# Split projections chunk by chunk, with retention between the attention projections, in a hybrid attention and mixture-of-experts block

## What is computed

```
mod = c @ w_ada + b_ada                 -> sh1, sc1, gt1, sh2, sc2, gt2
h   = rmsnorm(x) * (1 + sc1) + sh1
proj = h @ w_in                         # 1024 x 4688, columns:
   qa ka va (512 each), qi (1024), ki (64), wi (16), qb kb vb gb (512 each)
y_a: attention, 8 heads of 64; an indexer (16 heads: relu(qi.ki) weighted by wi) scores all keys,
     each query keeps its 256 best keys and takes a softmax over them
y_b: retention, 8 heads of 64: rotary q and k, decayed causal scores inside a tile, a state carried
     from tile to tile, group norm per head, times silu(gb)
x   = x + gt1 * (concat(y_a, y_b) @ w_o)
h   = rmsnorm(x) * (1 + sc2) + sh2
x   = x + gt2 * moe(h)                  # 32 experts in 4 groups, top 2; silu(h Wg) * (h Wu) @ Wd
out = rmsnorm(x)
```

## Time and profile before

| | |
|---|---|
| median of three runs | 1815.68 us |
| the profiled execution | 1816.96 us, its span 1815.1 us |
| busy: PE, DVE, ACT, POOL | 1577.2, 1083.7, 870.3, 273.1 us |
| mean granted TensorE clock | 0.932 of full speed |
| first float32 projection starts | 49.95 us |
| scoring starts | 186.7 us |
| second projections start | 290.1 us |
| last projection ends | 742.7 us |
| experts | from about 1090 us |

### The profile page before, as it was taken

The page is one execution under the profiler, slowest core; times in us unless marked ns, Lnnn a source line. Parts: engine busy times, 40 slices in busy tenths (PEclk is TensorE's granted clock), DMA queues, the critical chain, the costliest instruction groups (busy, mean ns, idle before and its releaser), DMA issues.

```text
span 1815.1 us, 20481 instructions
## 1 busy us (share of the span) xinstructions
PE 1577.2 (87%) x6918; PEld 1053.4 (58%) x6918; DVE 1083.7 (60%) x1498; ACT 870.3 (48%) x1181; POOL 273.1 (15%) x212
## 2 busy tenths in 40 slices
PE   2999899999999999867888984399999999999950
PEld 2446454444445555525666654378888888888840
DVE  6323796331233467353344424599999999999946
ACT  4000577778523300132344430177777777777722
POOL 0000010100021112100000000123232232323115
PEclk8899999999999999858999986599999999999985
DMA  9059743201100000321112110599999999999937
GB/s 375 16 189 376 269 154 136 81 4 44 47 6 7 6 7 12 110 85 47 59 61 69 42 47 23 196 390 397 405 401 400 399 398 397 398 395 399 385 142 275
DMA packets 85378, 346.97 MB, mean 191 GB/s; under 512 B 10048, under 2 KB 14272, under 8 KB 60736
## 3 DMA queue, kind: packets, MB, share of 16 engines
q1 hardware_dynamic: 56384, 268.51, 38.2%
q10 hardware_dynamic: 17024, 41.95, 6.0%
q0 software_dynamic: 11904, 35.66, 5.5%
HBM read 295.75 MB, written 58.72 MB: 195 GB/s over the span
## 4 chain that ended last, share of the span: by engine, by line
PE 79%; DVE 8%; ACT 3%; DMA 3%; issue 3%; POOL 2%; SPq 0%; DVEq 0%; POOLq 0%; ACTq 0%
PE PS L1522 16%; PE PS L1631 12%; PE PS L1470 11%; PE PS L1472 11%; PE PS L1471 11%; PE PS L1557 4%; PE PS L1760 2%; PE PS L1580 1%; PE PS L1656 1%; PE PS L1669 1%; DVE wlo L1393 1%; DVE WK L931 1%; PE PS L1735 1%; DMA WK<-in_w_ada 1%; PE PS L1542 1%
## 5 line engine op out<-in xcount | busy, mean ns | idle before, releaser
L1393 DVE TENSOR_TENSOR wlo<-raw,whi 128x2048 fp32r<-128x2048 f32 x192 | 435.7, 2284 | 34.0 <-ACT whi L844 33.6
L844 ACT ACTIVATE whi<-raw 128x2048 fp32r<-128x2048 f32 x192 | 363.8, 1913 | 116.6 <-DVE WK L1412 81.1
L1522 PE MATMUL PS<-BIG 128*128 128x512 f32 (+1 forms) x640 | 238.9, 528 | 1.1 <-ACT WK L726 1.1
L1631 PE MATMUL PS<-BIG 128*128 128x512 f32 x512 | 224.1, 599 | 0.7 <-ACT KV L713 0.7
L1470 PE MATMUL PS<-whi,xhi 128*128 128x512 f32 x512 | 203.9, 398 | 7.3 <-DVE wlo L1393 6.5
L1472 PE MATMUL PS<-whi,xlo 128*128 128x512 f32 x512 | 201.1, 393 | 0.0
L1471 PE MATMUL PS<-wlo,xhi 128*128 128x512 f32 x512 | 200.1, 391 | 0.0
L1522 PEld LDWEIGHTS PS<-BIG 128*128 128x128 f32 x640 | 110.2, 190 | 112.4 <-issue 110.5
L1631 PEld LDWEIGHTS PS<-BIG 128*128 128x128 f32 x512 | 97.6, 192 | 122.5 <-issue 120.3
L739 ACT ACTIVATE KV<-ACC,WK 128x1024 int8<-128x1024 f32 (+4 forms) x160 | 147.1, 923 | 31.3 <-DVE WK L1036 31.3
L617 POOL COPY wcol<-tw 128x1 f32 (+1 forms) x32 | 63.0, 1969 | 376.8 <-DVE WK L1430 376.8
(11 more groups left out here) (289 smaller groups left out, 2326.6 us busy)
## 6 DMA issues: line engine op xcount, KB each, us to landing
raw<-in_w_gate SPq DMA_DIRECT2D x64, 1024.0 KB, 7.1
raw<-in_w_up SPq DMA_DIRECT2D x64, 1024.0 KB, 7.8
raw<-in_w_down SPq DMA_DIRECT2D x64, 1024.0 KB, 7.4
y_dram<-zero ACTq DMA_DIRECT2D x8, 3072.0 KB, 13.9
BIG<-in_w_in SPq DMA_DIRECT2D x8, 2048.0 KB, 10.8
WK<-in_w_ada POOLq DMA_DIRECT2D x16, 1024.0 KB, 7.4
y_dram<-WK ACTq DMA_DIRECT2D x32, 512.0 KB, 6.7
BIG<-in_w_ada SPq DMA_DIRECT2D x3, 2048.0 KB, 18.5
```

The costliest lines, as they stand in the source:

```text
L844: nc.scalar.activation(whi[:, slot], raw[:, q], ACT.Copy).then_inc(G("m_hi"), 1)
L1393: V.tensor_tensor(wlo[:, slot], raw[:, q], whi[:, slot].bitcast(F32), ALU.subtract)\
L1522: last = mm(PS[:, u % 4, 0:w], hT[:, k, tile(t)], weights[:, k, 0:w], start=(k == 0), stop=(k == KD - 1))
L1631: last = mm(PS[:, k, :], hT[:, d, tile(t)], wb[k][:, d, :], start=(d == 0), stop=(d == KD - 1))
```

## The change

The input projections now all read split parts, except kiwi. hT is split once, in place (`hT_lo` over hT, `hT_hi` beside it). The chunks come in the order kiwi, qi0, qi1, then after scoring qb, kb, vb, gb, then qa, va, ka. Each chunk's 2 MB of weights are loaded, split by ACT (`split_high`) and DVE (`split_low`) in four pieces each at a fixed unit of the chunk before, and used by all 8 tiles. The retention inputs are finished per unit (rotated, or copied, or silu) into four buffers `EV` and stored to `b_dram`. Retention itself runs tile by tile in the 24 steps of qa, va and ka: three parts per tile (turn and evacuate; scores, kv and mask; values and finish), with its rows read back from `b_dram`. The counting steps of the key search spread over both stages, and its pieces are spent in the last 16 steps. Stores of qa rows move from POOL's queue to SP's. The late w_ada loads start after unit 16 rather than 8.

```diff
-CHUNKS_A = (("qi0", ...), ("qi1", ...), ("kiwi", 2560, 80), ("qa", ...), ("ka", ...), ("va", ...))
-CHUNKS_B = (("qb", 2640), ("kb", 3152), ("vb", 3664), ("gb", 4176))
+CHUNKS = (("kiwi", 2560, 80), ("qi0", 1536, 512), ("qi1", 2048, 512), ("qb", 2640, 512), ("kb", 3152, 512),
+          ("vb", 3664, 512), ("gb", 4176, 512), ("qa", 0, 512), ("va", 1024, 512), ("ka", 512, 512))
+INDEX, RETAIN, ATTEND = 0, 3, 7
+STEP_SPEND = 4.0
+        slots = [(WK[:, 5904:10000], WKR[:, 5904:10000], ACCR[:, 0:4096]), y_slot, y_slot, x_slot, y_slot, x_slot, y_slot,
+                 x_slot, (KV[:, 0:4096],) + x_slot[1:]]
+        def bank_of(u):
+            return u % 2 if u >= FIRST[ATTEND] else u % 4
 # SP
+            load_weights(0)
             ... w_ada loads ...
+            load_weights(1)
+            sp.wait_ge(G("xt_ready"), T)
+            load_weights(2)
+            sp.wait_ge(G("a_proj"), FIRST[RETAIN])
+            load_weights(3)
+            sp.wait_ge(G("sc_ready"), NU)
+            load_weights(4)
+            for n in range(RETAIN, ATTEND):
+                if n > RETAIN:
+                    sp.wait_ge(G("a_proj"), T * n)
+                    load_weights(n + 1)
+                for t in range(T):
...
+                    sp.dma_start(b_dram[n - RETAIN, tile(t), :], EV[m % 4]).then_inc(G(f"st_ev{m % 4}"), 16)
+            for step in range(3 * T):
+                t, part = divmod(step, 3)
+                if part == 2 and t < T - 1:
+                    sp.wait_ge(G("b_kv"), t + 1)
+                    load_rows("q", 0, t + 1)
+                    load_rows("k", 1, t + 1)
+                if part == 0 and t > 0:
+                    sp.wait_ge(G("b_y"), t)
+                    load_rows("v", 2, t)
+                    store_retained(t - 1)
+                    load_rows("g", 3, t)
+                if 1 <= step <= T:
+                    sp.wait_ge(G("a_evac"), TURN1 + step)
...                                                   # q_dram store
+                if step == T:
+                    sp.wait_ge(G("a_proj"), T * (ATTEND + 1))
+                    load_weights(ATTEND + 2)
 # ACT
+            def split_high(n):
+                act.wait_ge(G(f"ld_w{n % 3}"), 16 * (n // 3 + 1))
+                if n == ATTEND + 2:
+                    act.wait_ge(G("a_proj"), T * n)
+                raw_, _, hi = W[n]
+                for k in range(0, KD, 2):
+                    own.go(A(hi[:, k:k + 2], raw_[:, k:k + 2], ACT.Copy), G("w_hi"))
+            hidden_high(0)
+            for u in range(TURN1):
                 a_copy(u)
+                if u == 1:
+                    split_high(1)
+                if u == 3:
+                    hidden_high(1)
+                if u == T + 4:
+                    split_high(2)
...
+                if u == NU // 2:                      # inside scoring
+                    split_high(RETAIN)
...
+            for step in range(3 * T):
+                t, part = divmod(step, 3)
+                a_copy(FIRST[ATTEND] + step)
+                if part == 0:
+                    b_evacuate(t)
+                if step == 3:
+                    split_high(ATTEND + 1)
+                if step == 2 * T - 1:
+                    split_high(ATTEND + 2)
+                count_some(2)
 # DVE
             for m in range(TURN1):
                 a_rotate(m)
                 if m >= 1:
                     a_evacuate(m - 1)
+                if m == 2:
+                    split_low(1)
+                if m == 4:
+                    hidden_low(0)
+                if m == T + 1:
+                    hidden_low(1)
+                if m == T + 6:
+                    split_low(2)
...                                                   # scoring, then
+            split_low(RETAIN)
+            for u in range(FIRST[RETAIN], FIRST[ATTEND]):
+                n, t = divmod(u, T)
+                if n < RETAIN + 2:
+                    b_rotate(u)
+                if t == 4:
+                    split_low(n + 1)
+                narrow_some(1 + u % 2)
+            pieces = select()
+            for step in range(3 * T):
+                t, part = divmod(step, 3)
...
+                if name != "va":
+                    a_rotate(m)
+                narrow_some(2)
+                if step == 5:
+                    split_low(ATTEND + 1)
+                if step == 2 * T - 1:
+                    split_low(ATTEND + 2)
+                if (1 <= step <= T) or step > 2 * T:
+                    a_evacuate(m - 1)
+                if part == 1:
+                    b_mask(t)
...
+                if part == 2:
+                    b_finish(t)
+                if step >= T:
+                    spend(STEP_SPEND, pieces)
 # PE
+            def project(u):
...
+                    if t == 0 and k % 2 == 0:
+                        pe.wait_ge(G("w_lo"), 4 * (n - 1) + k // 2 + 1)
+                    _, w_lo, w_hi = W[n]
+                    last = split_product(out_, hT_hi[:, k, tile(t)], hT_lo[:, k, tile(t)], w_hi[:, k], w_lo[:, k],
+                                         first, final)
+            for step in range(3 * T):
+                t, part = divmod(step, 3)
+                m = TURN1 + (step if step <= T else step - T)
+                project(FIRST[ATTEND] + step)
+                if (1 <= step <= T) or step > 2 * T:
+                    a_turn(m - 1)
+                if step == 3 * T - 1:
+                    a_turn(m)
...
+                    query_keys(0, 0)
+                (retain_turn, retain_scores, retain_values)[part](t)
```

More of the change, by code:

```diff
@@ new lines, in _, with store_retained @@
+            sp.wait_ge(G("a_proj"), T * ATTEND)
+            load_weights(ATTEND + 1)
+            for j in range(4):
+                sp.wait_ge(G(f"st_ev{j}"), 16 * 8)
+            load_rows("g", 3, 0)
+            def load_queries(n):
+                sp.dma_start(queries(n), q_dram[:, :, tile(n)]).then_inc(G(f"ld_q{n % 2}"), 16)
+            def store_retained(t):
+                sp.wait_ge(G("b_out"), t + 1)
+                sp.dma_start(yb_dram[tile(t), :], WB["y"]).then_inc(G("st_yb"), 16)
@@ L697, in zero_rows, with hidden_high @@
                     .then_inc(G(f"st_y{h}"), 16)
+            def split_high(n):
[5 more added lines that the diff above has]
+                    own.go(A(hi[:, k:k + 2], raw_[:, k:k + 2], ACT.Copy), G("w_hi"))
+            def hidden_high(half):
+                part = slice(512 * half, 512 * half + 512)
+                for k in range(KD):
+                    act.wait_ge(G("hT_ready"), KD * half + k + 1)
+                    own.go(A(hT_hi[:, k, part], hT[:, k, part], ACT.Copy), G("hT_hi"))
             def a_copy(u):
-                name, _, w = CHUNKS_A[u // T]
+                name, _, w = CHUNKS[u // T]
                 t = u % T
@@ L994, in a_rotate, with split_low, hidden_low @@
                     own(rotate_part(v, t, 8), G("a_rot"))
+            def split_low(n):
+                raw_, lo, hi = W[n]
+                for k in range(0, KD, 2):
+                    dve.wait_ge(G("w_hi"), 4 * (n - 1) + k // 2 + 1)
+                    own.go(V.tensor_tensor(lo[:, k:k + 2], raw_[:, k:k + 2], hi[:, k:k + 2].bitcast(F32), ALU.subtract),
+                           G("w_lo"))
+            def hidden_low(half):
+                part = slice(512 * half, 512 * half + 512)
+                dve.wait_ge(G("a_proj"), 4 * half + 4)
+                for k in range(KD):
+                    dve.wait_ge(G("hT_hi"), KD * half + k + 1)
+                    own.go(V.tensor_tensor(hT_lo[:, k, part], hT[:, k, part], hT_hi[:, k, part].bitcast(F32),
+                                           ALU.subtract), G("hT_lo"))
             for m in range(TURN1):
@@ L1153, in b_retain, with b_mask @@
+            def b_mask(t):
                 dve.wait_ge(G("b_s"), t + 1)
@@ L1213, in _ @@
+            for _ in pieces:
+                pass
             for kind, i in order:
@@ L1534, in _ @@
-            a_project(range(NA1))
+            def project(u):
+                n, t = divmod(u, T)
+                w = CHUNKS[n][2]
+                out_ = PS[:, bank_of(u), 0:w]
+                if bank_before(u) is not None:
+                    pe.wait_ge(*evacuated(bank_before(u)))
+                if u == 0:
+                    pe.wait_ge(G("ld_w0"), 16)
+                for k in range(KD):
+                    first, final = k == 0, k == KD - 1
+                    if n == 0:
+                        if t % 4 == 0:
+                            pe.wait_ge(G("hT_ready"), KD * (t // 4) + k + 1)
+                        last = mm(out_, hT[:, k, tile(t)], W[0][:, k, :], start=first, stop=final)
+                        continue
+                    if n == 1 and t % 4 == 0:
+                        pe.wait_ge(G("hT_lo"), KD * (t // 4) + k + 1)
+                    if t == 0 and k % 2 == 0:
[3 more added lines that the diff above has]
+                                         first, final)
```

(6 more changed lines are left out.)

372 lines of the change are left out of this document (157 added, 215 removed).

## The result

The changed kernel takes **1749.28 us** (median of four executions, 1747.59 to 1750.48) where the kernel before took 1814.45 beside it: ratio 0.9642, 95% interval [0.9625, 0.9659]. The forecast was 1739, with four fifths of the chance between 1705 and 1773. The profiled execution took 1747.59 us, its span 1745.8.

What follows compares the result with a forecast made beforehand. TensorE's work was taken as the bound up to about 743 us. The last projection ending 56.6 us earlier and a tail 20.2 shorter gave -76.8; 1816.96 less 76.8 and 1.3 made 1739, with 1705 to 1773 leaving out a fifth.

Steps and rivals of the forecast that it cites:

- Rival 5: Wide projection units: three passes bring no gain at 0.286 us a pass, giving 1841 us; chance 0.01.
- rival 4: Attention part: short waits hold TensorE's clock down over its 24 units, costing 131 us, giving 1870; chance 0.04.
- the third case: Attention part: DVE and ACT coupled tighter, POOL lock added, about five tiles slip 5 us each: 1764; chance 0.19.
- Landmark 1: Start of scoring: first wide unit at 79.3, scoring from 176.6 us instead of 186.7, which is -10.1.
- the term of 2.8: Inside scoring: the new split_high stops ACT for 4.2 us, buffered rows cover 1.4, so +2.8 us (0 to 4.2).
- The 2.7 put on a cold restart: First b units after scoring: the idle stretch cools TensorE's clock, +2.7 us (0 to 2.7).
- Landmark 3: End of the last projection, after b chunks and attention part: 686.1 us instead of 742.7, with 26.6 of stalls.
- mask(4): Attention part: DVE's mask for retention tile 4 comes 5.3 us late for TensorE.
- Landmark 4: From last projection to first late row: 23 us (20 to 30) instead of 43.2, -20.2; after it 0.
- the first case: The forecast itself, stalls as worked: 1739 us, own range 1722 to 1752; chance 0.57.
- Rivals 2 and 3: Stalls around TensorE: mostly covered, 1710 us (chance 0.19), or DVE and ACT coupled tighter, 1764 us (chance 0.19).
- Rival 2: Scoring and attention part: stalls mostly covered, 3.5 us for 19.6 and several others nothing: 1710; chance 0.19.

Runs made afterwards that it cites:

- E4: Changed kernel with a fourth pass (low part of rows by low part of weights) in each wide unit: 1852.4 us, 1.0219 of the kernel before.
- E11: Changed kernel with one float32 product of the high parts in place of three passes, splits kept: 1821.09 us, 1.0046 of the kernel before.
- E1: Changed kernel with the eight zero stores moved into the b chunks, every third unit: 1740.69 us, 0.9578 of the kernel before.
- E7: Changed kernel with unused 128x512 float32 products ahead of and among the kiwi units: 1746.63 us, 0.9629 of the kernel before.
- E0: The changed kernel run again, unedited, as common ground for the experiments: 1748.41 us, 0.9639 of the kernel before.
- E2: Changed kernel with 2.5 instead of 4.0 nominal units of selection pieces per attention-projection step: 1730.17 us, 0.9538 of the kernel before.
- E3: Changed kernel with ACT's split of the first b weights behind scoring instead of in its middle: 1742.78 us, 0.9608 of the kernel before.
- E6: Changed kernel with the edits of E1, E2, E3 and no selection pieces ahead of chunk ka's split: 1722.53 us, 0.9490 of the kernel before.
- E9: E6 with the tile's mask ahead of DVE's two narrowing steps in the qa part: 1717.86 us, 0.9455 of the kernel before.
- E5: Changed kernel with all eight retention tiles in a stage of their own behind ka: 1788.16 us, 0.9840 of the kernel before.

## Why the prediction was right, and where it was not

**The unit.** 5.46 us from 24 passes of 0.227; measured 5.44. E4 and E11 price the term from both sides: 1.81 more a unit for the fourth pass, 73 us for all 72 units back to float32. Rival 5 is out, and so is rival 4: the clock was 0.99 in the b chunks and 0.93 in the attention part. A kb unit, beside which the third case had put the waits of DVE and POOL for each other, takes 5.44 as well. By the Trainium skill (TensorE: Matmul & The Clock Gate, "The HAM clock gate") activity releases the throttle; at 5.44 us a unit the trace agrees.

**Landmark 1 is the step that failed:** "176.6, which is -10.1" was 0.0. I counted for each new or moved instruction what it waits for, but took the unchanged ones as unchanged. The eight zero stores are not in the diff's arithmetic at all, yet they are tied to units that became 1.4 us shorter. E1 shows it by taking them away (6.2 us), E4 and E11 by lengthening the unit (their issues are short again). E1 leaves 3.9 of the 10.1: 1.3 at the first wide unit (80.6 there for 79.3) and 2.6 behind it, about 2 of them the cold start told below. The Trainium skill (DMA: Bandwidth & Descriptors, "Issuing engines are not separate DMA queues") calls the time an issue takes on its engine "usually small relative to the DMA itself". That holds for the kernel before (0.38 of a median 13.9 us from issue to landing); at 13.44 against 22.6 it doesn't, and the measurement decides.

The start within landmark 1 came out near, but for one reason more than I gave. I had kiwi done near 68, which needs the upper clock from about its third unit on, with DVE's chain setting 79.3. In fact kiwi ran at 0.50 throughout and TensorE itself was busy until 80.2. DVE's chain came out as worked (half of hT's low part 70.82 to 75.71, the rotation behind it done at 76.5), so the two nearly tied (TensorE waited for DVE for only 0.74 us, at 76.5), and with the clock up E7 shows DVE's alone at 77.7. The cold start of the first wide unit, about 2 us (clock 0.50 until 84.2), was missing. On the sentence about activity and the throttle this chunk is the exception: 28.71 us busy of 30 left the clock at 0.50.

**Scoring.** 110.8 from its start to the first qb unit, measured 111.0. That close a hit is luck: with the same code up to there E0 took 109.4 and E2 113.9. E3 confirms the term of 2.8 inside it. The 2.7 put on a cold restart there is not separated from it by any run.

**Landmark 3.** From the first qb unit to the last projection I had 398.7 us, 367.4 of work and 31.3 of stalls and clock. Measured 395.8: idle times sum to 18.1 (the three shown of that stretch and four under 0.8), and the other 10.3 are work at the lower clock (377.7 busy for 367.4). The parts were partly off. The gap at ka was 7.5 and not 12.4, as DVE's lag was smaller; mask(4) was 5.2 late for 5.3; the counts cost 3.7 for 3. E2 removes the one at mask(4), E6 halves the one at ka, and E9 moves the one from the counts. For the clock behind long gaps I had put 3; over this stretch E2 gave back 5.6 beside 5.4 of gaps.

**Landmark 4.** 19.1 us for 23, inside its range: values, finish and late rows overlap more than in my list. Behind it I had put 0, bound 3. The changed kernel's profiled execution takes 1033.2 us there for the 1029.2 of the kernel before, but E0, the same kernel, takes 1028.9. So the 0 stands within what moves between executions; why this stretch moves stays open. The clock was 0.50 from 710 to 750, and in the kernel before from 769 to 819.

**The sum.** 1749.28 is 10.3 over the forecast, about the 10.1 of landmark 1. It lies in the first case's own range of 1722 to 1752, near its end, and that is in part luck: the stores were no term of any case, and the range was made for other stalls. The other errors are smaller and cancel for the most part (+0.2, -2.9, -3.9 and, in this execution, +4.0).

**Rivals 2 and 3** asked whether TensorE or DVE and ACT set the time. E4 puts the share at 0.79 of what one adds to TensorE, E11 at 0.72 of what one takes off. It is mostly TensorE, with the order of DVE's and ACT's queues worth another 31 us (E9). Rival 2 had some 29 us for the same stalls, but as covered from the start; they were there, and it took edits to win most of them back. These edits change no work, only what stands ahead of what.

**Where the gain lies.** The 65 us are 73 from the passes less the 7 by which E11 is slower than the kernel before: what the new order brings, and what the splits, the cold kiwi chunk and the gaps at chunk changes cost, come out 7 us apart. No run takes the splits away alone, so the two sides are not known by themselves. Inside the new order, running the tiles between projections is worth 40 (E5); the kernel before had projections beside its tiles too, so this isn't a difference to before.

## What to carry to other kernels

Before shortening a repeated unit, list everything that is issued once per unit, transfers above all, and compare their rate with the new pace: an issue that backs up holds its engine's own work. A gap on TensorE is to be priced with the slow stretch behind it: here 1.4 us behind one of 4.97, and 5.6 for 5.4 us of gaps in E2. And where a second engine feeds the first in pieces, small edits to the order of its queue can be worth half of a change of arithmetic.

## What the hardware showed that I had not expected

- An issue of a transfer held ACT's queue for up to 13.44 us, when 3 MB stores came every 6.0 us (7.55 before two loads of 1 MB stood beside them); every 7.3 us they lasted 0.38 to 0.78.
- TensorE busy for 28.7 of 30 us with 80-column float32 products stayed at a granted clock of 0.50 the whole time. With 512-column products ahead of them and among them it was at 1.00 from 60 to 70 us (E7). Wide products between short narrow ones with pauses did not hold it (E8). What separates the two cases is open.
- Code that no edit touches varies between executions. From the start of scoring to the first qb unit it took 111.0 us (changed kernel), 109.4 (E0) and 113.9 (E2). Behind the last projection the clock stayed at 0.50 until near 750 in the changed kernel and in E0, but first rose near 730 in E1 and E3, whose last projections end 3.4 us earlier. A gain read in one profiled execution is uncertain by several us; the medians are less so.
